# Attention: the causal table is added by VectorE in place to the scores, instead of by products with the identity on TensorE

## The reference, cut to what matters

```python
# nsa, selected keys and window (8 heads of 64, 2 groups of keys): at 512 tokens
# 16 blocks of 64 keys are wanted and 8 exist, so both are causal attention over all keys
s = einsum(q, k) * scale
p_s = _masked_softmax(s, kpos <= t)          # and p_w likewise with its own keys
# fox (8 heads of 64): causal, with a bias of cumulated log forget gates
s = einsum(q, k) * scale + cq[..., None] - c[:, :, None, :]
p = _masked_softmax(s, kpos[None, :] <= t[:, None])
# memory (4 heads of 128, 256 keys): no mask
p = softmax(einsum(q, k) * scale)
```

## Time and profile before

| what | value |
| --- | --- |
| median of three runs | 3599.32 us |
| the profiled execution's own time | 3605.86 us |
| its span, from the first to the last instruction | 3604.1 us |
| busy: TensorE / its weight loads / VectorE / ScalarE | 90% / 58% / 39% / 27% of the span |
| mean granted clock of TensorE | 0.94 of full |
| fox stage, first and second layer | from about 2377 and 3110 us |
| nsa stage, first and second layer | from about 2472 and 3206 us, until about 2602 and 3337 us |

### The profile page before, as it was taken

One profiled execution on the slowest core, in us unless ns is written; L12 is line 12 of the kernel. 1 busy time (PEld: TensorE's weight loads), 2 busy tenths in 40 slices (PEclk: granted clock), 3 DMA queues, 4 the chain that ended last, 5 costly groups with the idle time before them and its releaser, 6 DMA issues. The chain is left out here.

```text
span 3604.1 us, 63938 instructions
## 1 busy us (share of the span) xinstructions
PE 3239.6 (90%) x25841; PEld 2108.3 (58%) x25842; DVE 1411.0 (39%) x2396; ACT 983.7 (27%) x1766; POOL 159.2 (4%) x222
## 2 busy tenths in 40 slices
PE   3998889887699999999999979987899899878998
PEld 2877687686333333333333338865588688655786
DVE  5546555556311111111111156454633464446333
ACT  2333313312111111111111112343522323435321
POOL 0000000001200000000000010000000000000000
PEclk8999999898699999999999979997999999979999
DMA  6621320324699998999999853231032133310331
GB/s 224 242 83 52 101 94 11 101 73 183 260 409 375 410 409 321 409 371 353 409 370 353 318 190 85 82 49 36 1 117 95 64 99 94 49 36 1 105 94 59
DMA packets 273123, 647.44 MB, mean 180 GB/s; under 512 B 36890, under 2 KB 97050, under 8 KB 270978
## 3 DMA queue, kind: packets, MB, share of 16 engines
q1 hardware_dynamic: 251314, 605.12, 46.2%
q0 software_dynamic: 6224, 21.24, 1.6%
q10 hardware_dynamic: 15360, 17.85, 1.5%
HBM read 600.88 MB, written 43.27 MB: 179 GB/s over the span
## 5 line engine op out<-in xcount | busy, mean ns | idle before, releaser
L1740 PE MATMUL ps<-raw,ex_xT 128*64 128x512 f32 x3072 | 677.9, 593 | 4.6 <-DMA raw<-in_w_dram 4.6
L1740 PEld LDWEIGHTS ps<-raw,ex_xT 128*64 128x64 f32 x3072 | 218.3, 137 | 419.1 <-issue 407.3
L1839 DVE TENSOR_SCALAR ex_gl<-ps 128x256 f32<-128x256 f32 x96 | 40.8, 425 | 948.8 <-PE ps L1740 948.8
L1740 PE MATMUL ps<-raw,ex_aT 128*64 128x512 f32 x1536 | 349.1, 596 | 3.3 <-DMA raw<-in_w_dram 3.3
L1740 PEld LDWEIGHTS ps<-raw,ex_aT 128*64 128x64 f32 x1536 | 105.5, 137 | 214.7 <-issue 207.1
L2000 PE MATMUL ps<-zhi,hl 128*128 128x512 f32 (+1 forms) x448 | 170.1, 380 | 0.0
L1999 PE MATMUL ps<-zlo,hh 128*128 128x512 f32 (+1 forms) x448 | 169.3, 378 | 0.0
L1998 PE MATMUL ps<-zhi,hh 128*128 128x512 f32 (+1 forms) x448 | 168.0, 375 | 0.2 <-DVE hl L2128 0.2
L2545 PE MATMUL ps<-uu_hi,hh 128*128 128x512 f32 x384 | 151.7, 395 | 10.6 <-DVE uu_lo L2657 10.6
L2547 PE MATMUL ps<-uu_hi,hl 128*128 128x512 f32 x384 | 152.3, 397 | 0.0
L2546 PE MATMUL ps<-uu_lo,hh 128*128 128x512 f32 x384 | 152.0, 396 | 0.0
(11 more groups left out here) (573 smaller groups left out, 5993.8 us busy)
## 6 DMA issues: line engine op xcount, KB each, us to landing
raw<-in_w_dram SPq DMA_DIRECT2D x384, 1024.0 KB, 18.5
oT<-in_w_in_dram SPq DMA_DIRECT2D x64, 512.0 KB, 3.6
u_raw<-in_w_in_dram SPq DMA_DIRECT2D x24, 1024.0 KB, 5.2
expert_out<-xn SPq DMA_DIRECT2D x4, 4096.0 KB, 16.5
expert_out<-ex_yrow ACTq DMA_DIRECT2D x98, 128.0 KB, 5.6
late_ada<-in_w_ada_dram SPq DMA_DIRECT2D x12, 1024.0 KB
early_w<-in_w_in_dram SPq DMA_DIRECT2D x10, 1024.0 KB, 13.7
mT<-in_w_ada_dram SPq DMA_DIRECT2D x4, 2048.0 KB, 19.9
```

The costliest lines, as they stand in the source:

```text
L1740: mm = pe.matmul(o, x, M["raw"][:, (slot + LATE_SLOTS) % RING, k, h * 512:(h + 1) * 512], start=(s >= 8 and kk == 0), stop=(kk == 7))
```

## The change

The causal table is added to the last 128 columns of both lanes' scores by one instruction of VectorE, which reads the two banks of PSUM and the table (repeated for both lanes) and writes the two banks in place, ahead of the maximum. VectorE waits for it before the maximum through `done`. The product with the identity goes from each lane's list, so that the product before it is the last of `score` and signals `scores`. Each unit carries a flag `causal`; memory units have it false. The tile `mask` and its two copies go.

```diff
             def maximum(i):
                 u = units[i]
                 dve.wait_ge(scores, i + 1)
+                if u["causal"]:
+                    last = ps[:, (i % 2) * 2:(i % 2) * 2 + 2, u["n"] - P:u["n"]]
+                    done(dve.tensor_tensor(last, last, bc(S("causal"), 1, 2), ALU.add))
                 done(dve.tensor_reduce(Z["mx"][:, i % 4, :], ps[:, (i % 2) * 2:(i % 2) * 2 + 2, 0:u["n"]], AX_X, ALU.max))
...
-        T["mask"] = sb(top, "mask", [P, 2, P], F32R)
         T["headrow"] = sb(top, "headrow", [P, 8], F32R)
         with stage(nc, "copied") as (block, copied):
             @block.vector
             def _(dve):
-                dve.tensor_copy(T["mask"][:, 0, :], ident).then_inc(copied, 1)
-                dve.tensor_copy(T["mask"][:, 1, :], T["s"]("causal")).then_inc(copied, 1)
                 dve.tensor_copy(T["headrow"][:, :], T["s"]("headrow")).then_inc(copied, 1)
-                dve.wait_ge(copied, 3)
+                dve.wait_ge(copied, 1)
...
-            def masked(i):
-
-                return T["mask"][:, 0, :], T["mask"][:, 1, :], i * P, (i + 1) * P
-
...
                                 "extra": [(Z["cc"][at, 0, i * P:n], pick.to_broadcast([HS, n]), 0, n),
-                                          (pick.to_broadcast([HS, P]), Z["cc"][at, 1, 0:n], 0, n), masked(i)],
+                                          (pick.to_broadcast([HS, P]), Z["cc"][at, 1, 0:n], 0, n)],
...
-                                "lanes": [{"q": Z["qT"][at, rr, i * P:n], "k": kT[at, 0:n], "extra": [masked(i)],
+                                "lanes": [{"q": Z["qT"][at, rr, i * P:n], "k": kT[at, 0:n], "extra": [],
```

More of the change, by code:

```diff
@@ L3018, in layer @@
                         n = (i + 1) * P
-                        unit = {"n": n, "gate": None, "out": c, "joint": None, "lanes": []}
+                        unit = {"n": n, "causal": True, "gate": None, "out": c, "joint": None, "lanes": []}
                         for side in range(2):
@@ L3053, in layer @@
                             units.append({
-                                "n": n, "gate": gates[:, i, rr, b, :], "out": rr, "joint": None,
-                                "lanes": [{"q": Z["qT"][at, rr, i * P:n], "k": kT[at, 0:n], "extra": [masked(i)],
+                                "n": n, "causal": True, "gate": gates[:, i, rr, b, :], "out": rr, "joint": None,
+                                "lanes": [{"q": Z["qT"][at, rr, i * P:n], "k": kT[at, 0:n], "extra": [],
                                            "v": [zb[:, kb, va + g * HS:va + (g + 1) * HS] for kb in range(i + 1)],
@@ L3061, in layer @@
                     for i in range(0, TT, 2):
-                        units.append({"n": 256, "gate": None, "out": 4 + h, "joint": ps[:, 6 + h % 2, i * P:(i + 2) * P],
+                        units.append({"n": 256, "causal": False, "gate": None, "out": 4 + h, "joint": ps[:, 6 + h % 2, i * P:(i + 2) * P],
                                       "lanes": [{"q": Z["mqT"][:, h, j * P:(j + 1) * P], "k": kmT[:, h, :], "extra": [],
```

## The result

The changed kernel takes 3642.81 us in the median of four runs (3634.05 to 3648.57), the kernel before on the same chip 3601.67. The ratio is 1.0114, with a 95% interval of 1.0098 to 1.0129: 41 us slower, between 35 and 46, or 1.1%. The forecast was 3638.6 us, 39.3 more. The profiled execution of the changed kernel took 3643.43 us with a span of 3641.7, which is 37.6 above the span before.

A forecast was written before the change was run, and what follows sets the result against it. The prediction took the loop between VectorE and ScalarE to bound the kernel. Additions +43.2 us, first units -2.5 and cycles held up by the clock -1.4 gave +39.3 on 3599.3: 3638.6 us, 1.1% slower, range 3624 to 3660.

The forecast's parts named there:

- The bound: Causal attention units: the loop between VectorE and ScalarE sets the pace in all but 4 of a layer's 48.
- The price of the addition: VectorE, 96 causal units: 420 ns each, 0.45 us with the step to the next instruction, +43.2 us in all.
- both bounds: Limits on the addition's price on VectorE: 291 ns below (+30.8 us in all), 685 ns above (+68.6 us).
- Its place: In VectorE's queue between the previous unit's scaling and the reduce, starting 0.53 us after the first scaling's start for n = 256.
- The first units: First unit of each of four attention stages: scores signalled 0.62 us earlier without mask products, -2.5 us in all.
- The cycles held up by TensorE at its lower clock: The nsa cycles: 2.7 us lost over both layers, of which half, -1.4 us, was counted as coming back.
- Rival B: TensorE idles more, its clock falls, and it becomes the bound in long attention units: 3671 us, chance 0.12.
- A: Rival: TensorE is the bound in attention, the addition hides and the mask products' 27 us come off: 3572 us, chance 0.02.
- C: Rival: VectorE's addition in PSUM costs up to 685 ns, so 43.2 us becomes 68.6: 3664 us, chance 0.07.
- the mix in which the two cancel: Mask products saved on TensorE and VectorE's addition nearly cancel: no change within 0.3%, chance 0.02.

The follow-up runs named there:

- experiment 1: The changed kernel without the addition, so no causal mask at all (no mask products either): 3597.66 us, ratio 0.9984 to the kernel before.
- experiment 4: The kernel before, products kept, with maximum(t) put ahead of normalise(t-1) in VectorE's queue: 3551.78 us, ratio 0.9862 to the kernel before.
- experiment 7: The kernel before with maximum(t) ahead of normalise(t-1) and the addition made besides the mask products: ratio 0.9912 to the kernel before.
- the fifth kernel: The changed kernel (addition, no mask products) with maximum(t) ahead of normalise(t-1) in VectorE's queue: ratio 0.9867 to the kernel before.

## Why the prediction was right

- **The bound.** The loop between VectorE and ScalarE sets the pace, TensorE stands beside it. Right: with the products gone the nsa cycle is unchanged to 0.02 us (experiment 1), and with the loop opened by the order of two lines it is 4.7 us shorter (experiment 4).
- **The price of the addition.** Forecast 0.42 us and 0.45 with the step to the next instruction. Measured 0.425, in all 96 units, and 0.465 with the step, so 1.4 us were missed of 44.6. That VectorE writes into PSUM, into two banks, costs some 5 ns at most: the row with the same number of elements out of PSUM was the right neighbour, and both bounds were far off. By the Trainium skill's formula of N + 151 cycles (page "VectorE: DVE Perf Modes", section on the TRN2 errata) the estimate was 424 ns, and the trace agrees with 425; by its table the estimate was 392 ns, and the trace doesn't agree.
- **Its place.** It starts where the reduce did, before the scaling has ended. Right. The memory units, which have no addition, are unchanged as forecast (18.94 us from their first reduce to their last, 18.95 before).
- **The first units,** 0.62 us each: right, in nsa 4.40 against 5.02, in fox 1.15 against 1.77.
- **The cycles held up by TensorE at its lower clock.** Half was counted as coming back, 1.4 us; all of it came, and the first fox cycles besides, 3.3 us. This term was mis-sized by 1.9 us, and this nearly cancels against the 1.4 us that were missed in the price. That the sum came out within half a microsecond of its parts as measured (39.3 against 38.8) is luck in that respect; without it the forecast would have been off by up to 2 us, which changes nothing in its direction.
- **Rival B, the clock,** is half right and came to nothing. The clock did fall more often (0.85 and 0.80 in cycles two and three). But no cycle is longer for it. The estimate of what a fall costs took TensorE at the lower level through all the long units; in the stretch shown the transposes and values of a long unit run at the lower level beside the scores of a short one (0.80 us), so TensorE had the time, and each unit of the loop had become 0.46 us longer. The Trainium skill's section on psum-queue depth-cycling (page "TensorE: Matmul & The Clock Gate") tells of repeated falls, and the trace agrees; it also tells of lost throughput, which the changed kernel's trace doesn't bear out (29.39 us at 0.80 as at 1.00) and that of experiment 7, with the loop opened, does (14.08 us at 0.87, 12.54 at 1.00).
- **Rivals A and C** fall: A, and with it the mix in which the two cancel, by experiment 1 and the longer cycles; C by the row of 425 ns.

The cycles came out at 13.91 and 29.39 us; 13.9 and 29.3 had been forecast. The total, 39.3, lies in the interval of 35 to 46 around the 41 us measured.

## What to carry to other kernels

Whether work should move from a busy engine to an idle one is not read from their busy shares (90% and 39% of the whole span here, 83% and 62% of the undisturbed nsa cycle in the earlier trace rows) but from who waits for whom in one turn of the loop: an engine that idles in the middle of a loop through itself has no time to give away. Look first at whether the loop can be opened by the order within a queue, here two lines and 50 us; only after that can it be told what an instruction costs on either engine. And waits summed over a cycle are no budget: in the fifth kernel they paid only for work in the same unit.

## What the runs showed of the hardware

A tensor_tensor of VectorE that reads and writes PSUM in place, over two banks, takes 425 ns for 256 float32 elements for each partition, 5 ns more than one that writes elsewhere, and the reduce behind it starts 0.46 to 0.47 us after its start, whether it follows a wait or another addition. And TensorE at its lower clock, for more of the time than before, cost nothing in cycles in which its work, at that clock, ended before it was wanted (29.39 us at mean clocks of 0.80 and 1.00); with the loop opened, where VectorE waits for its scores, it did (1.5 us in a fox cycle at 0.87).
